# Input projections of a two-block transformer: normalisation and rotation issued between the panels, values transposed in place

## The chip, the cores and the metric

One core of a Trainium2 chip. The metric is the device time of one launch in microseconds, the median of several runs.

## What is computed

Two blocks over 256 latent tokens of width 2048. The first block has two layers; each projects the latent tokens and 256 context tokens together, and its attention has two groups of eight heads, one with grouped keys (GQA) and one with latent vectors (MLA). The second block has a gated recurrence, a causal attention and a layer of retrieved experts, and isn't touched here. The part of the reference that matters:

```python
p = h @ w_in                       # (512 tokens, 2048) @ (2048, 4672)
q, k, v, g_gqa, cq, ckv, kr, g_mla = jnp.split(p, offsets, axis=-1)
q = rms_norm(q.reshape(B, S, 8, 128), q_gain)      # per head
k = rms_norm(k.reshape(B, S, 2, 128), k_gain)
v = v.reshape(B, S, 2, 128)
qm = rms_norm(cq, cq_gain) @ w_uq                   # over 512 channels
kvm = rms_norm(ckv, ckv_gain) @ w_ukv
# latent tokens alone: q, k, the rope part of qm, and kr
q, k, kr = apply_rope(q, ...), apply_rope(k, ...), apply_rope(kr, ...)
def rms_norm(x, g):  return x * rsqrt(mean(x * x) + 1e-6) * g
def apply_rope(x):   return concat([x1 * cos - x2 * sin, x2 * cos + x1 * sin])
```

The gates `g_gqa` and `g_mla` go through silu and are multiplied into the heads' outputs.

## The kernel before

Everything is kept transposed: channels on the 128 partitions, tokens along the row. Layer 0 works on all 512 tokens. Layer 1 needs queries and gates of the latent tokens alone, so its panels of `q`, `cq` and `g` are 256 tokens wide and those of `k`, `v`, `kr` and `ckv` 512.

**A panel** is 128 output channels of a projection: 16 weight tiles of 128x128 fp32, 1 MB. To keep fp32 accuracy in the fast fp32r form, weights and inputs are split into a high and a low part, and each tile is three matmuls (`w_hi` by `h_hi`, `w_hi` by `h_lo`, `w_lo` by `h_hi`), 48 for a panel. Two halves of a panel are converted one by one: ACT rounds half m into `w_hi` (`act_half`, L1270), VectorE subtracts to get `w_lo` (`dve_half`, L1276). There are four half buffers, so half m waits until TensorE is done with half m - 4. The panels themselves lie in a ring of two slots (`SLOTS`): SyncE starts the load of the next one when the second half of the slot's holder has been subtracted.

**The order** on ACT and VectorE is set by `paced`: before it turns to output number s it converts all halves up to 2s + 4, that is the first half of panel s + 2. Then `taken` does what belongs to output s: the eviction from PSUM once TensorE is done with the panel (VectorE if it is 512 wide from token 0, ACT if not), and on VectorE some chunks of modulation. A chunk (`ada_chunk`, L1689) is a product with 2048-wide rows of another 1 MB weight, loaded by GpSimd's queue into two buffers; it takes two passes for the first 64 chunks and one for the others. `spread` says how many chunks go behind which panel.

**The input projections** of a layer are one `gemm` stage of 37 panels: 0 to 7 are q, 8 and 9 k, 10 and 11 v, 12 kr, 13 to 16 cq, 17 to 20 ckv, 21 to 36 the gates. ACT evicts a gate with Silu into one of three buffers in `sq` and stores it in DRAM at once (L1318, L1320); the stage ends when all stores have landed. Behind the last panel TensorE transposes v (L994) into a buffer that lies over the projections' input, which isn't needed any more.

**The normalisation** is a stage of its own (`norm`), begun when the three engines are done with the projections. For each of 12 groups (8 q, 2 k, cq with four tiles, ckv with four) ACT squares each tile (L1344), TensorE sums over partitions with a matmul by ones (L1026), ACT takes Ln and Exp for the reciprocal root (L1353, L1354), and VectorE scales each tile (L1797). For each of 11 groups (q, k, kr) TensorE swaps the halves of a head by a matmul (L1136), and VectorE rotates (L1763 to L1766), two groups behind the scaling. Then the attention stage begins; its first matmuls are L1154.

## Time and profile before

| what | value |
|---|---|
| median of 3 runs | 3468.65 us (3468.17 to 3477.98) |
| profiled execution | 3465.94 us, span 3464.3 us |
| busy TensorE, VectorE, ACT, GpSimd | 87%, 72%, 33%, 18% of the span |
| chain that ended last, by engine | TensorE 54%, VectorE 17%, DMA 10%, weight loads 7%, issue 6% |
| largest lines of that chain | L1008 22% (and its weight loads 7%), L955 16% |

The shares are those of the whole execution, in which the touched stages are a part. So the rows below are taken from the stretches that the change touches: the input projections of layer 0 (124 to 529 us) and of layer 1 (1052 to 1330 us) and the stage behind each. In a timeline row the first number is the start, the second the duration; a note in square brackets is the idle time before it and who ended it. In a row of the windows stand the stretch, its length, the busy us (and instructions) of TensorE, its weight loads, VectorE, ACT and GpSimd, the granted clock, the DMA share and GB/s. A row of the chain has start and duration. TensorE's rows overlap, so the step between two starts is what counts there.

### The profile page before, as it was taken

How to read it: one execution, taken by the hardware profiler on the slowest of the kernel's cores; microseconds unless marked ns; L12 is line 12 of the kernel's file. 1: busy time of each engine (PE TensorE's matmuls, PEld its weight loads, DVE VectorE, ACT ScalarE, POOL GpSimd, SP SyncE). 2: the span in 40 equal slices, each digit the busy share in tenths (PEclk: the TensorE clock that was granted, in tenths of full speed). 3: DMA queues.
4: the chain of work that ended last, by engine and by line, in shares of the span. 5: the costliest groups of instructions: out<-in, count | busy, mean ns of one | idle time of the engine just before them, and what ended most of it. 6: DMA issues, size and time to landing. Idle time of an engine off the chain costs nothing.

```text
span 3464.3 us, 39039 instructions
## 1 busy us (share of the span) xinstructions
PE 2997.7 (87%) x14684; PEld 2299.3 (66%) x14684; DVE 2501.2 (72%) x3434; ACT 1155.4 (33%) x1751; POOL 610.3 (18%) x692
## 2 busy tenths in 40 slices
PE   5899997999989997999799998799999997454555
PEld 1588884546768885659699898788888886121222
DVE  7898975555767765547664545489898997789887
ACT  1311225323233234233553635344444443111101
POOL 1000000000000000000000000122222223777773
PEclk9999999999999999999899999999999999777777
DMA  9566661343766784437444353499999999899996
GB/s 405 203 246 244 261 261 42 117 187 125 288 231 231 297 310 158 158 117 278 179 159 152 128 200 139 154 417 415 402 418 403 418 395 391 331 410 402 409 410 279
DMA packets 149477, 932.67 MB, mean 269 GB/s; under 512 B 21552, under 2 KB 30000, under 8 KB 40880
## 3 DMA queue, kind: packets, MB, share of 16 engines
q0 software_dynamic: 77568, 520.24, 38.2%
q1 hardware_dynamic: 57616, 384.82, 28.1%
q10 hardware_dynamic: 14112, 25.17, 1.9%
q8 instruction: 117, 1.92, 0.2%
q14 instruction: 64, 0.52, 0.0%
HBM read 900.79 MB, written 29.36 MB: 269 GB/s over the span
## 4 chain that ended last, share of the span: by engine, by line
PE 54%; DVE 17%; DMA 10%; PEld 7%; issue 6%; POOL 3%; ACT 3%; DVEq 0%; ACTq 0%; SPq 0%; PEldq 0%; POOLq 0%
PE psum L1008 22%; PE psum L955 16%; PEld psum L1008 7%; PE psum L1015 5%; DVE psum L2106 4%; DMA memr<-in_panels_dram 4%; PE psum L1154 3%; DVE w_lo L1276 3%; DMA memh<-dots,memr 2%; PE psum L1171 2%; DVE junk L1689 2%; POOL memh L846 1%; POOL memr L858 1%; DMA memh<-in_panels_dram 1%; PE psum L1162 1%
## 5 line engine op out<-in xcount | busy, mean ns | idle before, releaser
L1276 DVE TENSOR_TENSOR w_lo<-memr,w_hi 128x1024 fp32r<-128x1024 f32 x614 | 736.8, 1221 | 387.2 <-ACT w_hi L1270 386.4
L1270 ACT ACTIVATE w_hi<-memr 128x1024 fp32r<-128x1024 f32 x614 | 640.9, 1056 | 936.5 <-DMA memr<-in_panels_dram 321.7
L1008 PE MATMUL psum<-h_hi,w_hi 128*128 128x512 f32 (+1 forms) x1664 | 591.1, 355 | 42.7 <-DVE w_lo L1276 27.9
L1008 PE MATMUL psum<-h_lo,w_hi 128*128 128x512 f32 (+1 forms) x1664 | 578.1, 347 | 0.0
L1008 PE MATMUL psum<-h_hi,w_lo 128*128 128x512 f32 (+1 forms) x1664 | 577.9, 347 | 0.0
L1689 DVE CUSTOM_DVE_ANT_0 junk<-memr 128x2048 bf16<-128x2048 f32 x224 | 512.2, 2287 | 76.4 <-DMA memr<-in_ada_dram 55.7
L1193 PE MATMUL psum<-memr,memh 128*128 128x512 f32 x480 | 254.2, 693 | 257.0 <-ACT memh L1627 204.4
L955 PE MATMUL psum<-w_hi,l_hi 128*128 128x512 f32 x1024 | 399.7, 390 | 14.6 <-DVE w_lo L1276 14.0
L955 PE MATMUL psum<-w_hi,l_lo 128*128 128x512 f32 x1024 | 398.9, 390 | 0.0
L955 PE MATMUL psum<-w_lo,l_hi 128*128 128x512 f32 x1024 | 398.9, 390 | 0.0
L1008 PEld LDWEIGHTS psum<-h_hi,w_hi 128*128 128x128 f32 x1664 | 320.0, 192 | 93.5 <-issue 33.0
L1193 PEld LDWEIGHTS psum<-memr,memh 128*128 128x128 f32 x480 | 105.0, 224 | 405.8 <-issue 208.9
L1008 PEld LDWEIGHTS psum<-h_lo,w_hi 128*128 128x128 f32 x1664 | 320.8, 193 | 40.5 <-issue 3.1
L1008 PEld LDWEIGHTS psum<-h_hi,w_lo 128*128 128x128 f32 x1664 | 320.7, 193 | 37.8
L827 POOL DMA_DIRECT2D memr<-in_ada_dram x160 | 84.5, 528 | 1463.3 <-DVE mod L1692 1453.6
L2106 DVE SCALAR_TENSOR_TENSOR psum<-memr,memh,psum 128x2048 f32<-128x2048 f32 x130 | 306.1, 2355 | 9.6
L1008 PE MATMUL psum<-l_hi,w_hi 128*128 128x256 f32 x912 | 266.1, 292 | 20.0 <-DVE l_lo L1778 15.2
L1008 PE MATMUL psum<-l_lo,w_hi 128*128 128x256 f32 x912 | 260.4, 286 | 0.0
L1008 PE MATMUL psum<-l_hi,w_lo 128*128 128x256 f32 x912 | 260.4, 286 | 0.0
L955 PEld LDWEIGHTS psum<-w_hi,l_hi 128*128 128x128 f32 x1024 | 192.6, 188 | 56.3 <-DVE w_lo L1276 15.8
L837 POOL DMA_INDIRECT memr<-in_peer_u_dram,memr x64 | 75.9, 1186 | 863.2 <-issue 611.5
L955 PEld LDWEIGHTS psum<-w_hi,l_lo 128*128 128x128 f32 x1024 | 192.7, 188 | 39.9
(243 smaller groups left out, 4326.3 us busy)
## 6 DMA issues: line engine op xcount, KB each, us to landing
memr<-in_panels_dram SPq DMA_DIRECT2D x323, 1024.0 KB, 7.5
memr<-in_ada_dram POOLq DMA_DIRECT2D x168, 1024.0 KB, 6.0
memh<-in_panels_dram SPq DMA_DIRECT2D x16, 1024.0 KB, 23.3
dots<-sq ACTq DMA_DIRECT2D x64, 256.0 KB, 9.9
memh<-in_ada_dram POOLq DMA_DIRECT2D x8, 1024.0 KB, 16.0
memr<-in_xin_dram SPq DMA_DIRECT2D x1, 4096.0 KB, 41.6
gstore<-sq ACTq DMA_DIRECT2D x16, 256.0 KB, 3.0
memh<-gstore SPq DMA_DIRECT2D x2, 2048.0 KB, 7.3
```

The costliest lines, as they stand in the source:

```text
L827: pool.dma_start(adar[:, s_, :], ada[i * 2 + s_]).then_inc(ada_in[s_], 16)
L837: pool.indirect_dma_start(out=early_rows[:, r % EARLY_SLOTS, :], out_offset=None, in_=(peer_u if j < TOPK else peer_v)[:, :], in_offset=ba ...
L955: ins = pe.matmul(bank(2 * (group % 2) + t), x_[:, kc, t * P:t * P + P], u_[:, c, :], start=kc == 0 and j == 0, stop=kc == DC - 1 and j == 2)
L1008: ins = pe.matmul(bank(o["bank"])[:, 0:o["w"]], w_[:, c, :], x_[:, kc, :], start=kc == 0 and j == 0, stop=kc == DC - 1 and j == 2)
L1015: ins = pe.matmul(bank(o["bank"])[:, a:b], lt, rh, start=j == 0, stop=j == len(pairs) - 1)
L1154: ins = pe.matmul(b[:, 0:nk], lt, rh, start=j == 0, stop=j == len(u["s"]) - 1)
L1171: ins = pe.matmul(bank(O_BANK + u["hn"] % 2)[:, u["col"]:u["col"] + P], u["v"][c], probT[:, u["n"] % 2, c * P:c * P + P], start=c == 0, st ...
L1193: ins = pe.matmul(bank(b), diags[:, q % DIAGS, :], row_views[r % NSLOT][:, 512 * b:512 * b + 512], start=first and i == 0, stop=(EARLY + m ...
L1270: act.activation(w_hi[:, m % HALVES, :, :], slot[:, 8 * i:8 * i + 8, :], ACT.Copy).then_inc(hi_ready, 1)
L1276: dve.tensor_tensor(w_lo[:, m % HALVES, :, :], raw_panel(o["g"])[0][:, 8 * i:8 * i + 8, :], w_hi[:, m % HALVES, :, :].bitcast(F32), ALU.su ...
L1689: chain(dve.tensor_tensor_reduce(junk[:, :], w, cact[:, v_, :], 1.0, 0.0, ALU.mult, ALU.add, mod[:, a, m:m + 1]))
L2106: dve.scalar_tensor_tensor(sums_dve, row, by, sums_dve, ALU.mult, ALU.add).then_inc(row_added, 1)
```

## The change

The stage of normalisation behind the input projections is taken out, and its work is issued inside the projections, by steps (the panel's number in the stage). For a tile made in panel i: ACT squares in step i + 1, TensorE sums in step i + 2 (behind panel i + 2), ACT takes the root in step i + 3, VectorE scales in step i + 4, TensorE swaps in step i + 5 and VectorE rotates in step i + 6. The swaps follow each other one step apart, and each waits for the rotation before it. With cq and ckv the last of the four tiles counts: roots in steps 19 and 23. The root now lies in PSUM (bank 5 or 7), the sums in bank 4, the swapped half in bank 6, where it is multiplied by the sine in place.

Buffers 0 and 1 of `sq` now hold squares during the projections, so all gates go through buffer 2. The two transposes of v follow kr's panel as outputs 13 and 14 of the stage and write v over the place it comes from. Modulation chunks: in layer 0's projections 48 instead of 50, with weight 1.0 for panels 0 to 16 and 1.4 for 17 to 34, and 32 instead of 30 in its output projection. Layer 1's spread is unchanged, but kr's chunks now come behind the second transpose. ACT preloads the table set of Ln and Exp at the end of the stage.

```diff
-        spread(DC, 50, [1] * 35 + [0] * 2)
+        spread(DC, 48, [1.0] * 17 + [1.4] * 18 + [0] * 2)
-        spread(DC + 44, 30, [1] * 14 + [0] * 2)
+        spread(DC + 44, 32, [1] * 14 + [0] * 2)
...
+                        for n in range(totals["gate"], totals["gate"] + (2 if "dense" in o else 1)):
+                            gate_slot.append(n % 3 if "dense" in o else 2)
+                            gate_use.append(gate_slot[:-1].count(gate_slot[-1]))
...
+        def inside(st, groups, panels_of):
+            st["inside"] = groups
+            for step, o in enumerate(o for o in st["outs"] if "x" in o):
+                o["step"] = step
+            by_step = [o for o in st["outs"] if "x" in o]
+            swap_at = 0
+            for gr, made in zip(groups, panels_of):
+                gr.update(sq0=totals["sq"], ms=totals["ms"], sw=totals["swap"], made=[by_step[i] for i in made])
+                ready_at = made[-1]
+                if gr.get("stat", True):
+                    gr["square_at"] = [i + 1 for i in made]
+                    gr["sum_at"] = [i + 2 for i in made]
+                    gr["root_at"] = made[-1] + 3
+                    gr["scale_at"] = ready_at = made[-1] + 4
+                    totals["sq"] += len(gr["x"])
+                    totals["ms"] += 1
+                if "rope" in gr:
+                    gr["swap_at"] = swap_at = max(ready_at, swap_at) + 1
+                    gr["rope_at"] = swap_at + 1
+                    totals["swap"] += 1
...
-            v = region(HL, 4, 2, P)
+            v = region(AR + 5120, 2, 4, P)
...
+                turns = [dict(turn=[vT[:, b, P * t:P * t + P] for t in range(4)], after=[outs[-2], outs[-1]],
+                              eng="VA"[b], dst=v[:, b, :, :], view="p (t d) -> p t d", act=ACT.Copy)
+                         for b in range(2)] if kind == "kr" else []
+                return [o] + turns
...
-            norm(groups)
+            inside(st, groups, [range(i, i + 1) for i in range(10)] + [range(12, 13), range(13, 17), range(17, 21)])
...
+        SUM_BANK, SWAP_BANK = 4, 6
+        def root_of(gr):
+            return bank(5 + 2 * (gr["ms"] % 2))[:, 0:gr["x"][0].shape[-1]]
...
+        def pe_inside(pe, st, step):
+            for gr in st["inside"]:
+                for j, at in enumerate(gr.get("sum_at", ())):
+                    if at != step:
+                        continue
+                    n, w = gr["sq0"] + j, gr["x"][j].shape[-1]
+                    if j == 0 and gr["ms"]:
+                        pe.wait_ge(rinv_ready, gr["ms"])
+                    pe.wait_ge(sq_ready, n + 1)
+                    pe.matmul(bank(SUM_BANK)[:, 0:w], ones[:, :], sq[:, n % 2, 0:w], start=j == 0,
+                              stop=j == len(gr["x"]) - 1).then_inc(sq_used, 1)
+                if gr.get("swap_at") == step:
+                    if gr["sw"]:
+                        pe.wait_ge(roped, gr["sw"])
+                    if gr.get("stat", True):
+                        pe.wait_ge(normed, gr["ms"] + 1)
+                    else:
+                        pe.wait_ge(evac[gr["made"][0]["eng"]], gr["made"][0]["ev"] + 1)
+                    pe.matmul(bank(SWAP_BANK)[:, 0:S], con("swap2" if gr["pair"] else "swap", P), gr["rope"],
+                              start=True, stop=True).then_inc(swapped, 1)
...
+        def act_inside(act, st, step, chain):
+            for gr in st["inside"]:
+                for j, at in enumerate(gr.get("square_at", ())):
+                    if at != step:
+                        continue
+                    n, x = gr["sq0"] + j, gr["x"][j]
+                    act.wait_ge(evac[gr["made"][j]["eng"]], gr["made"][j]["ev"] + 1)
+                    if n >= 2:
+                        act.wait_ge(sq_used, n - 1)
+                    act.activation(sq[:, n % 2, 0:x.shape[-1]], x, ACT.Square).then_inc(sq_ready, 1)
+                if gr.get("root_at") == step:
+                    act.wait_ge(sq_used, gr["sq0"] + len(gr["x"]))
+                    if gr["ms"] >= 2:
+                        act.wait_ge(normed, gr["ms"] - 1)
+                    r = root_of(gr)
+                    chain(act.activation(r, bank(SUM_BANK)[:, 0:r.shape[-1]], ACT.Ln, bias=eps_t[:, :], scale=1.0 / gr["w"]))
+                    act.activation(r, r, ACT.Exp, scale=-0.5).then_inc(rinv_ready, 1)
...
-                if "gate" in o and o["gate"] >= 3:
-                    act.wait_ge(g_out[o["gate"] % 3], 16 * (o["gate"] // 3))
+                if "gate" in o and gate_use[o["gate"]]:
+                    act.wait_ge(g_out[gate_slot[o["gate"]]], 16 * gate_use[o["gate"]])
...
+            if "inside" in st:
+                act.preload_act_table_set("natural_log_exp_and_others")
...
+        def dve_inside(dve, st, step, chain):
+            for gr in st["inside"]:
+                if gr.get("scale_at") == step:
+                    dve.wait_ge(rinv_ready, gr["ms"] + 1)
+                    for x, gain in zip(gr["x"], gr["gain"]):
+                        ins = dve.scalar_tensor_tensor(x, x, col(*gain), root_of(gr), ALU.mult, ALU.mult)
+                    ins.then_inc(normed, 1)
+                if gr.get("rope_at") == step:
+                    x, t = gr["rope"], bank(SWAP_BANK)[:, 0:S]
+                    cos, sin = ("cos2", "sin2") if gr["pair"] else ("cos", "sin")
+                    dve.wait_ge(swapped, gr["sw"] + 1)
+                    dve.tensor_tensor(t, t, con(sin, S), ALU.mult)
+                    chain(dve.tensor_tensor(x, x, con(cos, S), ALU.mult))
+                    dve.tensor_tensor(x, x, t, ALU.add).then_inc(roped, 1)
```

## Rows read from the trace of the kernel before

**Rows 1.** Windows of the projections and the stage behind them, layers 0 and 1
```profile
124.00:529.00 405.00, 404.80 (x1780) 334.80 (x1781) 340.13 (x365) 98.14 (x115) 26.39 (x50) 1.00 0.61 230
529.00:574.00 45.00, 27.37 (x65) 11.04 (x62) 25.82 (x52) 27.18 (x45) 0.00 (x0) 0.90 0.14 53
1052.00:1330.00 278.00, 263.30 (x1729) 242.31 (x1730) 191.41 (x207) 81.15 (x98) 22.16 (x42) 0.98 0.78 297
1330.00:1371.00 41.00, 23.06 (x68) 12.84 (x66) 22.20 (x51) 21.12 (x45) 0.00 (x0) 0.87 0.23 90
```

**Rows 2.** Waits of TensorE in layer 1's projections: us, times, longest
```profile
PE psum L1008 <- DVE w_lo L1276: 16.4, 20, 3.7
```

**Rows 3.** Timeline about layer 0's normalisation stage, TensorE and ACT
```profile
528.63 1.03 PE L994 MATMUL psum<-consts,memr 128*128 128x128 f32 x8
...
531.70 1.28 ACT L1368 ACT_TABLE_LOAD   x1 [1.21 <-DMA gstore<-sq]
...
574.03 3.75 PE L1154 MATMUL psum<-memr 128*128 128x256 f32 x6 [7.45 <-DVEq L2163]
```

**Rows 4.** Timeline and chain of waits about layer 1's normalisation stage
```profile
1329.97 1.03 PE L994 MATMUL psum<-consts,memr 128*128 128x128 f32 x8
1330.64 4.43 DMA gstore<-sq
...
1371.61 5.46 PE L1154 MATMUL psum<-memr 128*128 128x512 f32 x6 [6.10 <-DVEq L2163]
```

**Rows 5.** Timeline of TensorE, sums inside the output projections of both layers
```profile
983.10 1.02 PE L918 MATMUL psum<-sq,ones 128*128 128x512 f32 x2
...
994.88 1.02 PE L918 MATMUL psum<-sq,ones 128*128 128x512 f32 x2
...
1575.43 0.59 PE L918 MATMUL psum<-sq,ones 128*128 128x256 f32 x2
...
1581.61 0.59 PE L918 MATMUL psum<-sq,ones 128*128 128x256 f32 x2
```

**Rows 6.** Chain of waits: 35 panels of layer 0, one of 256 columns
```profile
147.99 380.82 PE psum L1008 x1680
...
1814.53 5.75 PE psum L1008 x48
```

**Rows 7.** Chain of waits in layer 1's gate panels
```profile
1237.17 9.30 DMA memr<-in_panels_dram
...
1252.43 8.23 DMA memr<-in_panels_dram
1260.69 1.07 ACT w_hi L1270
1261.78 1.23 DVE w_lo L1276
1263.01 2.20 DVE junk L1689
1265.46 1.14 DVE w_lo L1276
```

**Rows 8.** Timeline of the work in layer 0's normalisation stage
```profile
541.21 0.42 DVE L1763 TENSOR_TENSOR memr<-memr,consts 128x256 f32<-128x256 f32 x1
...
542.46 0.75 DVE L1797 SCALAR_TENSOR_TENSOR memr<-memr,cols 128x512 f32<-128x512 f32 x1
```

**Rows 9.** Timeline of TensorE and ACT in layer 1's projections
```profile
1079.13 1.06 ACT L1270 ACTIVATE w_hi<-memr 128x1024 fp32r<-128x1024 f32 x1 [6.52 <-DMA memr<-in_panels_dram]
...
1094.10 0.40 PE L1008 MATMUL psum<-h_hi,w_hi 128*128 128x512 f32 x1
...
1099.42 1.06 ACT L1270 ACTIVATE w_hi<-memr 128x1024 fp32r<-128x1024 f32 x1 [8.66 <-DMA memr<-in_panels_dram]
...
1161.06 0.38 PE L1008 MATMUL psum<-h_hi,w_hi 128*128 128x256 f32 x1 [3.74 <-DVE w_lo L1276]
```

**Rows 10.** Line L1320, the stores of layer 1's gates
```profile
DMA to landing us min/median/max: 1.7/5.4/7.7
```

More of the change, by code:

```diff
@@ L307, in gemm @@
                         o["gate"] = totals["gate"]
[L308 removed]
+                        for n in range(totals["gate"], totals["gate"] + (2 if "dense" in o else 1)):
+                            gate_slot.append(n % 3 if "dense" in o else 2)
+                            gate_use.append(gate_slot[:-1].count(gate_slot[-1]))
+                        totals["gate"] = len(gate_slot)
                     o.update(g=g, n=totals["out"], bank=totals["out"] % 4, ev=totals[o["eng"]],
@@ L710, in _ @@
                     n_gates = sum("gate" in o for s_ in stages[:st["k"]] for o in s_.get("outs", ()))
-                    for i in range(3):
-                        sp.wait_ge(g_out[i], 16 * ((n_gates + 2 - i) // 3))
+                    for i in sorted(set(gate_slot[:n_gates])):
+                        sp.wait_ge(g_out[i], 16 * gate_slot[:n_gates].count(i))
                     sp.dma_start(st["x"], gstore.rearrange("p (c t) -> p c t", c=DC)[:, c0:c1, :]).then_inc(g_in, 16)
@@ L929, in pe_gemm @@
                 pe_output(pe, o, st["norm"]["groups"][0]["xl"] if p_ == 0 and "norm" in st else None)
+                if "step" in o:
+                    pe_inside(pe, st, o["step"])
                 if "sums" in st and p_ >= 2:
@@ L1129, in stats @@
                     pe_stats(pe, gr)
-            def swap(gr):
-                if gr["sw"] >= 2:
-                    pe.wait_ge(roped, gr["sw"] - 1)
-                if gr.get("stat", True):
-                    pe.wait_ge(normed, gr["ms"] + 1)
-                pe.matmul(bank(6 + gr["sw"] % 2)[:, 0:S], con("swap2" if gr["pair"] else "swap", P), gr["rope"],
-                          start=True, stop=True).then_inc(swapped, 1)
-            for i in range(len(gs) + 2):
-                if i < len(gs) and gs[i].get("stat", True):
-                    stats(gs[i])
-                if i >= 2 and "rope" in gs[i - 2]:
-                    swap(gs[i - 2])
+            for gr in gs:
+                stats(gr)
         def pe_attend(pe, st):
@@ L1284, in taken @@
                 p_ = o["n"] - st["outs"][0]["n"]
+                if "step" in o:
+                    act_inside(act, st, o["step"], chain)
                 if p_ < len(st.get("split", ())):
@@ L1300, in taken @@
                         n = o["gate"] + t
-                        if n >= 3:
-                            act.wait_ge(g_out[n % 3], 16 * (n // 3))
-                        ins = act.activation(gate_st[:, n % 3, :], bank(2 * (o["dense"] // 4 % 2) + t), ACT.Copy)
+                        if gate_use[n]:
+                            act.wait_ge(g_out[gate_slot[n]], 16 * gate_use[n])
+                        ins = act.activation(gate_st[:, gate_slot[n], :], bank(2 * (o["dense"] // 4 % 2) + t), ACT.Copy)
                     ins.then_inc(evac["A"], 1)
@@ L1316, in taken @@
                 if "store" in o:
-                    dst = gate_st[:, o["gate"] % 3, a0:a1]
+                    dst = gate_st[:, gate_slot[o["gate"]], a0:a1]
                     act.activation(dst, src, o["act"]).then_inc(evac["A"], 1)
                     act.wait_ge(evac["A"], o["ev"] + 1)
-                    act.dma_start(o["store"], dst).then_inc(g_out[o["gate"] % 3], 16)
+                    act.dma_start(o["store"], dst).then_inc(g_out[gate_slot[o["gate"]]], 16)
                     return
@@ L1335, in act_gemm @@
             if n_gates:
-                for i in range(3):
-                    act.wait_ge(g_out[i], 16 * ((n_gates + 2 - i) // 3))
+                for i in sorted(set(gate_slot[:n_gates])):
+                    act.wait_ge(g_out[i], 16 * gate_slot[:n_gates].count(i))
         def act_squares(act, gr):
@@ L1368, in act_norm @@
             act.preload_act_table_set("natural_log_exp_and_others")
-            gs = [gr for gr in st["groups"] if gr.get("stat", True)]
+            gs = st["groups"]
             def squares(gr):
@@ L1719, in taken @@
             def taken(o):
+                if "step" in o:
+                    dve_inside(dve, st, o["step"], chain)
                 if o["eng"] == "V":
@@ L1811, in scale @@
                     ins.then_inc(normed, 1)
-            for i in range(len(gs) + 2):
-                if i < len(gs) and gs[i].get("stat", True):
-                    scale(gs[i])
-                if i >= 2 and "rope" in gs[i - 2]:
-                    if gs[i - 2].get("stat", True):
-                        dve.wait_ge(normed, gs[i - 2]["ms"] + 1)
-                    rotate(dve, gs[i - 2], chain)
+            for gr in gs:
+                scale(gr)
         def dve_attend(dve, st, chain):
```

21 lines of the change are left out of this document (7 added, 14 removed).

## The prediction

> **What bounds the kernel now.** I read the page's chain first (its shares stand in the table above): matmuls of `pe_output` (L1008) lead it, so the dense projections are bound by TensorE. Then the windows of the four stretches that the change touches: the input projections of layer 0 and 1 and the normalisation stage behind each [rows 1]. In layer 0's projections TensorE is busy in 404.8 of 405 us: nothing hidden is missing there, and whatever is added to TensorE adds to the time. In layer 1's it is busy in 263.3 of 278, and the waits name who is late: `w_lo` of VectorE, 16.4 us in 20 waits [rows 2]. In the two normalisation stages no engine is full: they are a relay of small work between ACT, TensorE and VectorE.
>
> The timeline gives their length. Layer 0: the first transpose of v (the end of the last panel) starts at 528.63, attention's first matmul at 574.03, so 45.4 us [rows 3]. Layer 1: 1329.97 to 1371.61, so 41.6 us [rows 4].
>
> **What is removed.** Without the stage, attention starts when ACT has stored the last gate. In layer 0 that store had landed at 531.70, when ACT went on to the stage's table load [rows 3]; with 0.2 us for the stage's end attention would start 3.3 us behind the last panel: 45.4 - 3.3 = 42.1 us gone. In layer 1 the store is issued at 1330.64 and takes 4.43 us [rows 4], so 5.3 us behind: 36.3 us gone. Sum 78.4 us.
>
> **What TensorE gets between the panels.** A sum of squares 512 wide inside a stream of panels can be seen in layer 0's output projection: sums at 983.10 and 994.88, a period of 11.78 us [rows 5]. A panel of 512 columns without one is 380.82 / 35 = 10.88 us [rows 6]. So 0.90 us for each. With 256 columns: period 6.18, plain panel 5.75 or 5.76 [rows 5, 6], so 0.42. A swap (256 wide, also fp32) isn't seen in a stream; I take the same 0.42, with bounds 0.3 and 0.9.
> Layer 0: 18 sums x 0.90 = 16.2; 11 swaps x 0.42 = 4.6; 8 transposes of v, which were hidden behind the last gate's store and now lie between panels, 1.0 [rows 3]. Together 21.8 us. Layer 1: 8 + 4 sums x 0.42 = 5.0; 2 + 4 sums x 0.90 = 5.4; swaps 4.6; transposes 1.0. Together 16.0 us; 1.8 of it (the sums of steps 21, 22) falls where TensorE waits anyway, so 14.2.
>
> **The new waits.** At the end of each panel `pe_inside` waits: the sum of panel s-2 for the root that ACT computes in step s, and the swap for the rotation that VectorE does in step s. Both engines do that behind the conversion of half 2s+4, which is the first half of panel s+2 and can't begin before panel s is half through. Before, TensorE could be some 1.5 panels ahead of the conversions; now it can't leave panel s before half 2s+4 is converted. Queued behind the waiting matmul is the whole next panel.
> The chain from mid-panel: round 1.07, subtract 1.14 to 1.23 [rows 7], the rotation, from 541.21 to 542.46 us three operations that overlap to 1.25 [rows 8], handovers 0.3: 3.8 to 4.3 us, and another 0.7 if the scaling comes first. In layer 0 half a panel is 5.44 us: it fits with about a microsecond over, if VectorE is free. There it does two subtractions 2.4, an eviction 0.7 (taken like the 0.75 of a scaling [rows 8]), scaling and rotation 2.0, and 1.14 modulation chunks per panel. One pass is 2.45 us from start to next start [rows 7], two passes 4.8, so 5.5: 10.6 of the 12.2 us that a panel now takes. Before it had 1.43 chunks; the lighter first weights are what makes this fit. Rounding gives panels 3, 10, 17 and 18 two chunks. Only panel 10's meets a swap: in step 11 VectorE comes to its subtractions 9.0 us into the panel and ends the rotation at 13.2, against 10.88: a stall of 2.3 us. ACT was busy in 98 of 405 us [rows 1] and gets some 2 us a panel more: not full. Bounds 0 and 8.
> The two chunks moved to layer 0's output projection (one pass each) cost 4.9 us of VectorE over 14 panels. It works there (2.4 + 1.0 + 5.5 + 0.9) of 11.78 us, so nothing; uncovered, 4.9.
> **Layer 0: -42.1 + 21.8 + 2.3 = -18.0 us.**
>
> **Layer 1** is tighter, because a query panel is 5.76 us and half of it, 2.88, is less than the 4-us chain. The panel ring has two slots, too: a load goes out when the second half of a panel is subtracted, lands in 8.23 or 9.30 us, then round 1.07, subtract 1.23, chunk 2.45, subtract 1.14 [rows 7]: 14.2 us for two panels, 15.3 at 9.30. In the query panels this ring already lags behind TensorE: panel 8 starts at 1094.10, but ACT rounds half 18 (step 7's) at 1099.42, having waited for the panel's load [rows 9]. Today that is free, since the wide panels behind let it catch up. With the new waits TensorE pays it. I moved the stretch step by step, with panel loads of 7 to 8.4 us. Step 4: half 12's load is there at 1079.13 as before [rows 9], rounded at 1080.2, square 0.4, root 0.9, so 1081.5; panel 4, two sums of 0.42 later than before, ends at 1077.7: stall 3.8. Step 6: its panel ends at 1094.4, the rotation (half 16 subtracted at 1093.9) at 1095.2: 0.8. Step 7: panel's end 1101.9; half 18's load, begun at 1091.5, lands at 1099.9, rounded, subtracted and rotated 1103.4: 1.5. So 6.1 us up to panel 8. Among the wide panels 8 to 11 the chain fits. Into step 12 VectorE comes late by panel 11's three chunks (7.4 and some 3 for their loads): 2.8. In step 13 it has two more chunks and half 30 first and rotates 10.9 us after panel 13 began, which takes 5.8: 5.1. Steps 14 and 15, alike with one chunk and none: 0.7 and 1.9. Against that the `w_lo` wait of 3.74 us in panel 14, 5.5 with what follows from it [rows 9], goes: the two transposes are outputs of their own, `paced` converts one more half ahead of the first, and the chunks hang on the second. So 6.1 + 10.5 - 5.5 = 11.1 us to panel 17. Bounds: 0 - 5.5, if loads land early, and 25, if they land at 9 us.
> In the gate panels the ring is the bound [rows 7], so each delay of VectorE or ACT shows. Step 23 gives ACT a root and two table loads (1.28 each [rows 3]), step 24 gives VectorE four scalings, 2.7. Some 1.4 us of the first is slack: I take 3.
> The gates now use one buffer of `sq` instead of three, so each waits until the one before has landed. In layer 1 a store lands in 1.7 to 7.7 us, median 5.4 [rows 10], and gates are some 6.8 us apart with 0.8 of it gone for eviction and issue. About a quarter of the stores are late, by up to 1.7: I take 1, and 1.5 more at the end, where two gates come close together. In layer 0 gates are 10.9 us apart: nothing.
> **Layer 1: -36.3 + 14.2 + 11.1 + 3 + 2.5 = -5.5 us.**
>
> On the switches between Silu and Ln the row shows 1.28 us for a load and work right behind it. The Trainium skill (ScalarE: Activation LUTs, What ACT_TABLE_LOAD costs) speaks against the change here: it gives about 2.66 us for each switch, with a drain, and its section on table sets says to batch calls by set, which the change breaks up. By that rule layer 1 would lose 2.8 us more; by the rows it loses what I took.
>
> **Clock.** In the two removed stretches the granted clock was 0.90 and 0.87 of full, against 1.00 and 0.98 in the projections before them [rows 1]. So attention now starts behind dense work at 2.4 GHz, not behind a sparse stretch partly at 1.2: 0.5 us for each layer, an estimate between 0 and 2.
>
> **Sum.** -18.0 - 5.5 - 1.0 = -24.5 us. The profiled execution took 3465.94 us (span 3464.3), 2.7 under the median of 3468.65, so 3441.4 on its scale and 3444.2 on the median's: 3444.
>
> **The rivals.**
> *A: the new waits are free, 0.2.* The ring recovers in the longer panels, and VectorE's order hides the rotations. Layer 0: -42.1 + 21.8 = -20.3. Layer 1: -36.3 + 14.2 - 5.5 + 3 = -24.6. With the clock -46, so 3423, or up to 3432 with a few stalls. For it: VectorE was busy in only 191 of 278 us of layer 1's projections [rows 1]. Against it: a half panel of 2.88 us can't hold a 4-us chain.
> *B: layer 1 gives back all of the gain, 0.17.* If loads land at 9 us all along, its stalls are 25 instead of 11 and the gate panels lose 5 more: -24 + 14 + 5 = -5, so 3464, or from 3452 on with half of it. For it: loads of 8.23 and 9.30 us in the chain [rows 7]. Against it: the added 14 us of TensorE work are themselves slack for the loads.
> *C: slower than before, 0.04.* The single gate buffer decides. If stores in layer 1 landed later than (6.8 - 0.8) = 6.0 us as a rule, each of 15 gates would pay the excess and the kernel would be tied to store, evict, store. From a landing of 7.6 us on, 1.6 x 15 = 24 eats the gain; at 8.5 it is 2.5 x 15 = 38, and 3444 + 38 = 3482. For it: a longest landing of 7.7 [rows 10]. Against it: the median is 5.4.
> *D: the change doesn't do what it says, 0.02:* a stage is still waited for. 3468.
>
> The forecast keeps 0.57. Range: 3425 (most of A) to 3459 (half of B); what is left out is the rest of both, C and D, 0.2. A difference of 0.3% (10.4 us, about what a measurement can tell) lies at 3458.2: faster 0.84, same 0.12, slower 0.04.
>
> **What would show it.** In the profile after: no L1026 or L1136 row behind the last panel of either layer; attention's first matmul 3 to 4 us behind layer 0's last panel, 5 to 7 behind layer 1's; panels with a sum 0.90 or 0.42 us longer; in layer 1 waits of the new matmuls for ACT's root and VectorE's rotation in steps 4, 6, 7 and 12 to 15, of 15 to 20 us in all, and no wait of 3.74 in panel 14; layer 0's with one such wait of 2 us near step 11. I am wrong if these waits are missing (A), or if the last gate of layer 1 ends more than 35 us later than before relative to its first panel (B, C).

## The result and the profile after

The changed kernel took 3450.37 us (median of 4 runs, 3446.20 to 3451.03) against 3470.86 (3468.17 to 3477.98): ratio 0.9934, 95% interval 0.9921 to 0.9946, so 23 us or 0.66% less; 3444 within 3425 to 3459 was forecast. The profiled execution took 3450.2 us (span 3448.5, before 3464.3).

Windows of the changed kernel: layer 0's projections and what lies between them and attention, then layer 1's from its panel 1 on (columns as in [rows 1]).
```profile
124.00:554.00 430.00, 427.71 (x1842) 346.70 (x1842) 360.82 (x411) 126.32 (x162) 25.34 (x48) 0.99 0.56 212
554.00:557.00 3.00, 0.45 (x1) 0.45 (x2) 0.00 (x0) 1.70 (x2) 0.00 (x0) 0.92 0.23 87
1036.80:1344.00 307.20, 284.66 (x1794) 257.77 (x1794) 212.53 (x258) 103.41 (x144) 22.18 (x42) 0.97 0.70 268
1344.00:1351.00 7.00, 0.32 (x2) 0.23 (x2) 0.00 (x0) 1.67 (x2) 0.00 (x0) 0.82 0.60 239
```
The stretches of 45 and 41 us of [rows 1] have shrunk to 3 and 7. In layer 0's projections TensorE is still busy in all but 2.3 us, with more instructions in a longer stretch. In layer 1's it is idle for 22.5 of 307.2 us, where it was for 14.7 of 278, and the granted clock is 0.97 where it was 0.98.

The waits of TensorE from panel 1 of layer 1 to attention name who is late (us, times, longest), to be laid beside [rows 2]:
```profile
PE psum L1058 <- DVE w_lo L1315: 13.0, 16, 3.2
PE psum L952 <- DVE memr L1837: 8.2, 6, 2.8
PE psum L1193 <- ACTq L1736: 6.7, 1, 6.7
PE psum L943 <- ACT psum L1335: 3.1, 1, 3.1
```
Two waits are new: the swap (L952) for VectorE's rotation, and a sum of squares (L943) for ACT's root. The waits for `w_lo` fell by 3.4: the one of 3.74 us in panel 14 [rows 9] isn't there.

Timeline of TensorE, starts of attention in layers 0 and 1:
```profile
556.55 3.66 PE L1193 MATMUL psum<-memr 128*128 128x256 f32 x6 [2.83 <-ACTq L1736]
...
1350.78 2.07 PE L1193 MATMUL psum<-memr 128*128 128x512 f32 x2 [6.68 <-ACTq L1736]
```
From the first projection matmul to attention layer 0 went from 449.8 us (124.2 to 574.03) to 432.1 (124.47 to 556.55): -17.7, forecast -18.0. From panel 1 to attention layer 1 went from 319.4 (1052.25 to 1371.61) to 314.0 (1036.79 to 1350.78): -5.4, forecast -5.5. Attention of layer 1 starts 20.8 us earlier. That is 2.3 less than the two gains together: the first projection matmul comes 0.3 later, and from layer 0's attention to panel 1 of layer 1 it takes 480.2 us instead of 478.2. Of these 2.0 us 1.7 lie in one place. In both kernels TensorE waits 2.02 us behind layer 0's first heads; the 10 us after it read, in the kernel before and in the changed one:
```profile
641.00:651.00 10.00, 9.95 (x23) 4.48 (x24) 1.89 (x3) 2.78 (x5) 0.00 (x0) 1.00 0.00 1
```
```profile
623.50:633.50 10.00, 10.00 (x20) 4.35 (x21) 1.89 (x3) 2.29 (x5) 0.00 (x0) 0.83 0.00 0
```
The granted clock is 1.00 in the one and 0.83 in the other, behind the same wait. Why isn't shown.

The profiled execution ends 15.8 us earlier, so 5 more us came back behind layer 1's attention, in work that is the same in both. VectorE's instructions there, laid side by side, are 21.1 us earlier at 2219 us of the kernel before, 19.4 at 2971 and 15.7 at the end: most of it goes in the last 500 us. These are two single executions; the two medians differ by 20.5, and the ratio gives 23. The cause was not traced.

The new waits are visible one by one. VectorE and then TensorE at the end of layer 1's step 12:
```profile
1145.15 2.29 DVE L1751 CUSTOM_DVE_ANT_0 junk<-memr 128x2048 bf16<-128x2048 f32 x1 [3.41 <-DMA memr<-in_ada_dram]
...
1147.62 2.35 DVE L1315 TENSOR_TENSOR w_lo<-memr,w_hi 128x1024 fp32r<-128x1024 f32 x2
1149.89 0.42 DVE L1835 TENSOR_TENSOR psum<-psum,consts 128x256 f32<-128x256 f32 x1
...
1150.67 0.42 DVE L1837 TENSOR_TENSOR memr<-memr,psum 128x256 f32<-128x256 f32 x1
```
```profile
1151.14 1.22 PE L952 MATMUL psum<-memr,consts 128*128 128x256 f32 x2 [2.83 <-DVE memr L1837]
1152.16 1.91 PE L1044 MATMUL psum<-consts,memr 128*128 128x128 f32 x8
1153.72 0.56 PE L1058 MATMUL psum<-h_hi,w_hi 128*128 128x256 f32 x1
```
Read it downwards: VectorE waits 3.41 us for a chunk's load, does the chunk of step 11, then both subtractions of step 12, and only then the rotation; TensorE stands 2.83 us before the swap. And the swap takes 1.22 us here. In layer 0, without a wait ahead of it, the same two instructions read:
```profile
282.54 0.59 PE L952 MATMUL psum<-memr,consts 128*128 128x256 f32 x2
282.97 1.04 PE L1044 MATMUL psum<-consts,memr 128*128 128x128 f32 x8
```
Behind this wait TensorE works at 1.2 GHz instead of 2.4. That price wasn't in the forecast.

### The profile page after: what moved, and what is told of

Read it like the earlier page. It is cut to its first block, busy times and chain, and to the rows that moved or that the text cites. A ratio compares the mean times of both kernels' runs of the same rounds, so it can differ in the third digit from the quotient of the medians.

```text
span 3448.5 us, 39045 instructions
## 1 busy us (share of the span) xinstructions
PE 2988.6 (87%) x14684; PEld 2303.8 (67%) x14684; DVE 2498.5 (72%) x3434; ACT 1160.9 (34%) x1757; POOL 605.8 (18%) x692
## 4 chain that ended last, share of the span: by engine, by line
PE 55%; DVE 17%; DMA 10%; PEld 7%; issue 5%; POOL 3%; ACT 2%; DVEq 0%; ACTq 0%; SPq 0%; PEldq 0%; POOLq 0%
PE psum L1058 22%; PE psum L1005 16%; PEld psum L1058 7%; PE psum L1065 6%; DVE psum L2181 4%; DMA memr<-in_panels_dram 4%; DVE w_lo L1315 4%; PE psum L1193 3%; DVE junk L1751 2%; DMA memh<-dots,memr 2%; PE psum L1210 2%; DMA memh<-in_panels_dram 1%; POOL memr L884 1%; POOL memh L872 1%; PE psum L1201 1%
## 5 line engine op out<-in xcount | busy, mean ns | idle before, releaser
L1058 PE MATMUL psum<-h_hi,w_hi 128*128 128x512 f32 (+1 forms) x1664 | 605.0, 364 | 39.5 <-DVE w_lo L1315 24.7
L1005 PE MATMUL psum<-w_hi,l_hi 128*128 128x512 f32 x1024 | 400.0, 391 | 15.3 <-DVE w_lo L1315 14.7
L2181 DVE SCALAR_TENSOR_TENSOR psum<-memr,memh,psum 128x2048 f32<-128x2048 f32 x130 | 306.1, 2355 | 10.7 <-DVE psum L2181 1.4
L1058 PE MATMUL psum<-l_hi,w_hi 128*128 128x256 f32 x912 | 266.5, 292 | 19.4 <-DVE l_lo L1858 14.7
L1005 PEld LDWEIGHTS psum<-w_lo,l_hi 128*128 128x128 f32 x1024 | 192.8, 188 | 40.2
## 6 DMA issues: line engine op xcount, KB each, us to landing
memh<-in_panels_dram SPq DMA_DIRECT2D x16, 1024.0 KB, 23.6
```

What stands on the lines that cost most here:

```text
L1005: ins = pe.matmul(bank(2 * (group % 2) + t), x_[:, kc, t * P:t * P + P], u_[:, c, :], start=kc == 0 and j == 0, stop=kc == DC - 1 and j == 2)
L1058: ins = pe.matmul(bank(o["bank"])[:, 0:o["w"]], w_[:, c, :], x_[:, kc, :], start=kc == 0 and j == 0, stop=kc == DC - 1 and j == 2)
L2181: dve.scalar_tensor_tensor(sums_dve, row, by, sums_dve, ALU.mult, ALU.add).then_inc(row_added, 1)
```

## The experiments

"Inside work" stands for all that the change inserts between the panels: squares, sums, roots, scalings, swaps and rotations. The first column of numbers is the ratio to the kernel before, on the same chip; the second is the distance of that ratio from the changed kernel's 0.9934, times 3470 us (the two 95% intervals together make it uncertain by 6 to 8 us, so a distance of less says nothing by itself); the third is when layer 1's attention starts in the profiled execution, against 1350.78. The last four runs were on a chip on which the kernel before took 3511 to 3515 us, so only ratios go across.

| run | ratio (95%) | us from the changed kernel | layer 1's attention, us |
|---|---|---|---|
| changed kernel | 0.9934 (0.9921 to 0.9946) | 0 | 1350.78 |
| inside work first, both engines | 0.9883 (0.9869 to 0.9898) | -17.7 | -14.2 |
| no inside work | 0.9782 (0.9768 to 0.9796) | -52.7 | -51.0 |
| old weights of layer 0's chunks | 0.9965 (0.9953 to 0.9977) | +10.8 | +10.2 |
| three gate buffers | 0.9928 (0.9915 to 0.9941) | -2.1 | -2.8 |
| transposes late | 0.9929 (0.9915 to 0.9942) | -1.7 | +0.2 |
| fewer chunks in layer 1 | 0.9923 (0.9909 to 0.9937) | -3.8 | +3.0 |
| gates without Silu | 0.9930 (0.9916 to 0.9944) | -1.4 | 0.0 |
| together | 0.9895 (0.9880 to 0.9910) | -13.5 | -13.6 |
| VectorE's inside work first | 0.9905 (0.9891 to 0.9919) | -10.1 | -9.8 |
| ACT's inside work first | 0.9937 (0.9924 to 0.9949) | +1.0 | -1.1 |
| thin spread | 0.9866 (0.9851 to 0.9881) | -23.6 | -17.8 |
| best | 0.9854 (0.9836 to 0.9872) | -27.8 | -25.9 |

**What the inside work costs.**
```diff
-            for gr, made in zip(groups, panels_of):
+            for gr, made in ():
```


> The squares, sums, roots, scalings, swaps and rotations of queries, keys and latent vectors are left out; nothing takes their place, so attention works on vectors that are neither normalised nor rotated. The two transposes and the gate buffer stay as they are. This measures what the inserted work and its waits cost together. Theory (my terms): layer 0 20.8 for the matmuls and 1.8 for the stall, layer 1 13.2 and 11 + 3 for waits: 50 us less than the changed kernel, 3400 us. Rival (part of the inserted work in layer 1 fills time in which TensorE would wait for the panel ring): waits for w_lo grow by 8 us or more and the time is 3408 to 3415.

3394.8 us, with normalisation and rotation left out altogether. In the trace layer 0 is 23.3 us shorter (408.8 from first matmul to attention), against 22.6 by my terms. Together with layer 1, attention there starts 51.0 us earlier; expected was 50. TensorE's waits in layer 1:
```profile
PE psum L1058 <- DVE w_lo L1315: 18.4, 18, 4.6
PE psum L1193 <- ACTq L1736: 7.1, 1, 7.1
```
Waits for `w_lo` do grow (18.4 against 13.0), as the rival had it, yet not enough to eat the gain. The longest, 4.6 us, stands in panel 14, where the kernel before has its 3.74, although the transposes of v lie ahead of it.

**The order inside a step.** The squares, roots, scalings and rotations of a step are issued ahead of the two conversions of the step.
```diff
-        def paced(st, part, taken):
+        def paced(st, part, taken, first=None):
...
             for o in st["outs"]:
+                if first is not None and "step" in o:
+                    first(o["step"])
                 while j < min(2 * split + (5 if "x" in o else 4), len(halves_)):
...
-                if "step" in o:
-                    act_inside(act, st, o["step"], chain)
```
(and the same on VectorE; `first` calls `act_inside` and `dve_inside`.)

> The order on ACT and VectorE alone is changed: in each step squares, roots, scalings and rotations come before the two half-panel conversions of the step, not behind them. Theory (the stalls of the new matmuls come from standing behind the conversion of half 2s+4): the 1.6 us wait in layer 0's step 11 goes, and of the 11.3 us of waits for the root and the rotation in layer 1's steps 4, 6 to 8 and 12 to 16 at least 8 go; 3439 to 3443 us against 3450. Rival (in layer 1 the ring of panel loads is late anyway): the same time comes back as waits for the subtracted half (w_lo), the sum of TensorE's waits in layer 1's projections stays within 3 us of what it was, 3447 to 3450. Second rival: ACT, which now first waits for the end of a panel, converts halves later, and the time grows to 3453 or more.

3432.0 us against 3469.65: 17.7 us less, more than the theory's 7 to 11. Waits of TensorE from panel 1 of layer 1 on:
```profile
PE psum L1058 <- DVE w_lo L1317: 12.0, 13, 2.3
...
PE psum L952 <- DVE memr L1837: 5.4, 3, 4.0
```
The wait for the root is gone, the waits for the rotation fell from 8.2 to 5.4, and layer 0's from 1.55 to none. That is 5.9 us in layer 1 where at least 8 were expected, as one of 4.0 us, in step 13, is new. Yet from panel 1 to panel 17 layer 1 takes 139.8 us instead of 149.8, 10.0 less for 5.9 of waits: they had cost more than their length.

Each engine's half alone:

> Of the order that gave 3432 us only VectorE's half: scalings and rotations come ahead of its two subtractions, while ACT squares and takes roots behind its conversions as in the changed kernel. Theory (the rotation behind the subtraction of half 2s+4 is the larger part of the stalls): the waits for VectorE of 8.2 us in layer 1 and 1.6 in layer 0 fall to under 3, the wait of 3.1 us for ACT's root in step 4 stays, 9 to 13 us less than the changed kernel: 3437 to 3441. Rival (the lateness sits on ACT, whose conversions VectorE waits for in either order): 5 us less at most, 3445 or more.

> The other half alone: squares and roots ahead of ACT's conversions, VectorE as in the changed kernel. Theory: the 3.1 us wait of step 4 and part of the 3.2 us wait for w_lo behind step 23's root go, the waits for the rotation stay; 3 to 6 us less: 3444 to 3447. Rival (ACT's order is the larger part): 9 us less or more, 3441 or below.

Waits in layer 1 with VectorE's inside work first, and then with ACT's:
```profile
PE psum L952 <- DVE memr L1838: 5.0, 3, 4.0
PE psum L943 <- ACT psum L1337: 3.3, 1, 3.3
```
```profile
PE psum L1058 <- DVE w_lo L1317: 12.9, 15, 3.0
PE psum L952 <- DVE memr L1838: 12.6, 6, 3.6
```
VectorE's half gives 10 of the 18 us, as expected, though its waits for the rotation fell to 5.0 and not under 3. ACT's half alone gives nothing that can be told (0.9937), where 3 to 6 us were expected and 9 by its rival: the root comes in time, but VectorE then stands behind the same subtractions, and a wait of 3.6 us for the rotation, at the end of step 6, takes the place of the 3.1 for the root. The lateness is passed on: moving ACT's work ahead gains only where VectorE's is ahead too (attention of layer 1 starts 4.4 us earlier with both than with VectorE's alone).

**The chunks ahead of a rotation in layer 0.**
```diff
-        spread(DC, 48, [1.0] * 17 + [1.4] * 18 + [0] * 2)
+        spread(DC, 50, [1] * 35 + [0] * 2)
-        spread(DC + 44, 32, [1] * 14 + [0] * 2)
+        spread(DC + 44, 30, [1] * 14 + [0] * 2)
```


> Only the spread of layer 0's modulation chunks is put back to what it was before (50 chunks evenly over 35 panels, 30 in the output projection). Panels 5, 8, 10 and 12 then have two chunks and are followed by a swap. Theory (VectorE with two chunks ends the rotation 13 us into a panel of 10.9): stalls of 1.6 to 2.3 us in steps 6, 9, 11 and 13 instead of in step 11 alone, layer 0 longer by 5 to 7 us: 3455 to 3457. Rival (a late rotation in one step is made up by slack, or the two chunks in the output projection cost as much): no difference, within 2 us of the changed kernel. Second rival (with 1.43 chunks a panel VectorE is full and its lag adds up): 10 us or more, 3460.

10.8 us slower than the changed kernel, attention of layer 0 at 567.41. Waits of TensorE in layer 0's projections:
```profile
PE psum L952 <- DVE memr L1837: 7.4, 4, 2.7
PE psum L943 <- ACT psum L1335: 2.5, 1, 2.5
```
The four waits for the rotation are where the theory put them (steps 6, 9, 11, 13: 1.6, 1.6, 1.6, 2.7). A fifth, 2.5 us for the root in step 3, nobody had forecast, and the waits' 9.9 us against 1.6 cost 10.9. So the size lies at the second rival's, its mechanism (a lag that adds up) isn't seen. The run changes the number of chunks (50 for 48) together with their weights, so it doesn't tell which of the two counts.

**The chunks ahead of a rotation in layer 1.**
```diff
-        spread(DC + 44, 32, [1] * 14 + [0] * 2)
-        spread(DC + 60, 42, [0.6] * 8 + [2] * 5 + [0.6] * 4 + [2] * 4 + [0.8] * 14 + [0] * 2)
+        spread(DC + 44, 38, [1] * 14 + [0] * 2)
+        spread(DC + 60, 36, [1, 0, 1, 1, 0, 1, 1, 0, 2, 2, 2, 1] + [0] * 4 + [1, 2, 2, 3, 2] + [1] * 14 + [0] * 2)
```


> Six modulation chunks are taken out of layer 1's input projections (panels 7 and 11 to 15: two, one, one, none, none, none there instead of more) and put into layer 0's output projection, 38 instead of 32 over 14 panels. Theory (VectorE comes late to the rotations because of the chunks ahead of them): the waits of 2.8 us in step 12 and 2.5 in step 14 go, 4 to 6 us less: 3444 to 3447, and layer 0's output projection, with 11.0 us of VectorE in 11.8, pays nothing. Rival (the stalls come from the order behind the conversion, whatever VectorE does in between; or VectorE is full in the output projection): within 2 us of the changed kernel, or slower.

Waits of TensorE in layer 0's output projection and the first pair of layer 1 (850 to 1050 us), and then of the swap in layer 1's projections:
```profile
PE psum L1058 <- DVE w_lo L1315: 9.4, 6, 2.3
```
```profile
PE psum L952 <- DVE memr L1837: 3.6, 5, 0.7
```
The time can't tell this run from the changed kernel, and layer 1's attention starts 3.0 us later. In layer 1 alone the theory holds: no wait for a rotation over 0.72 us, and from panel 1's `w_lo` wait to attention it takes 308.9 us instead of 314.0. But the place I moved the chunks to wasn't free: the changed kernel has 1.9 us of such waits between 850 and 1050, this one 9.4, and layer 1 begins 8.1 us later. My sum of 11.0 us of VectorE in 11.8 counted VectorE's work and left out its waits for the chunks' loads: from 850 to 1000 us they are 32.2 us, against 22.6 in the changed kernel.

**The transposes.** They go back behind the last panel.
```diff
-                turns = [dict(turn=[vT[:, b, P * t:P * t + P] for t in range(4)], after=[outs[-2], outs[-1]],
...
             st = gemm(g, 37, in_proj)
+            add(st, [dict(turn=[vT[:, b, P * t:P * t + P] for t in range(4)],
+                          after=[o for o in st["outs"] if o["g"] - g in (10, 11)],
```

> The two transposes of the values stand behind the last gate panel again (as before the change, but still in place); all else is the changed kernel. The prediction held that moving them ahead takes away the 3.74 us wait of layer 1's panel 14 (one more half is converted ahead, the chunks hang on the second transpose). By that theory the wait returns: 3.7 to 5.5 us more in layer 1, less the 1 us of transposes in each layer that hide behind the last store again: 3452 to 3454. Rival: the run without the inside work had a wait of 4.61 us at that place although the transposes stood ahead, so it is the waits for the rotation in steps 12 to 15 that took its place; then nothing returns, and the time is that of the changed kernel or up to 2 us less: 3448 to 3451.

The rival's case: 0.9929, and no wait for `w_lo` of 3.74 us in panel 14. The waits of layer 1:
```profile
PE psum L1059 <- DVE w_lo L1316: 13.9, 17, 3.3
PE psum L953 <- DVE memr L1838: 9.7, 6, 2.8
```
The 3.74 us aren't removed by the place of the transposes.

**The gate buffers.**
```diff
-                            gate_slot.append(n % 3 if "dense" in o else 2)
+                            gate_slot.append(n % 3 if "dense" in o else o["slot"])
...
-                    o.update(store=..., eng="A", act=ACT.Silu)
+                    o.update(store=..., eng="A", act=ACT.Silu, slot=2 if i < 3 else i % 3)
```


> The gates from the fourth on use all three buffers again (by then no squares are left), the first three the single one. Theory (the last gates of layer 1 are tied to store, eviction, store): ACT's waits for a gate's store, 12 us in 4 waits, go but for those of the first gates, attention starts 5.5 us after the end of the last panel instead of 7.5, and the waits for w_lo in the gate panels shrink by 1 to 3 us: 3 to 5 us in all, 3445 to 3447. Rival (only the last store counts, and it lands no earlier): within 1 us of the changed kernel.

The end of the chain of waits before layer 1's attention in the changed kernel (start, duration):
```profile
1329.31 7.07 DMA gstore<-sq
...
1336.82 4.88 DMA gstore<-sq
...
1342.13 6.42 DMA gstore<-sq
...
1348.99 1.70 DMA gstore<-sq
```
Store, eviction, store, four times. With three buffers ACT waits for TensorE there, not for a store:
```profile
1343.28 0.38 ACT L1378 ACTIVATE sq<-psum 128x256 f32<-128x256 f32 x1 [6.08 <-PE psum L1058]
```
Attention starts 2.8 us earlier in the trace. The ratio (2.1 us less, give or take 6) can't tell that from nothing; the place and the mechanism are shown, the size is just below the theory's 3 to 5.

**The table loads.**
```diff
-                    o.update(store=..., eng="A", act=ACT.Silu)
+                    o.update(store=..., eng="A", act=ACT.Copy)
```


> The gates are stored without Silu (Copy in its place), so ACT never leaves the table set of Ln and Exp in the projections; attention then multiplies by the raw projection. This takes the three table loads of step 23 in each layer and those at the first gate and at the end away: 5 of 1.28 us for each layer. Theory (ACT is late at step 23 and TensorE waits 3.2 us for the half that it converts next): that wait shrinks to under 1 us, 2 to 4 us less, all of it in layer 1: 3446 to 3448. Rival (a slower ring alone makes that wait): within 1 us. By the Trainium skill (ScalarE: Activation LUTs, What ACT_TABLE_LOAD costs), at 2.66 us a switch, it would be 4 to 6 us.

ACT about layer 1's step 23, changed kernel:
```profile
1256.98 1.28 ACT L1334 ACT_TABLE_LOAD   x1
1258.28 0.66 ACT L1334 ACTIVATE psum<-psum,eps_t 128x512 f32<-128x512 f32 x1
1258.96 1.28 ACT L1335 ACT_TABLE_LOAD   x1
1260.25 0.58 ACT L1335 ACTIVATE psum<-psum 128x512 f32<-128x512 f32 x1
1260.85 1.28 ACT L1378 ACT_TABLE_LOAD   x1
...
1262.99 1.06 ACT L1309 ACTIVATE w_hi<-memr 128x1024 fp32r<-128x1024 f32 x1 [0.46 <-ACT sq L1378]
1264.52 1.06 ACT L1309 ACTIVATE w_hi<-memr 128x1024 fp32r<-128x1024 f32 x1 [0.48 <-DMA memr<-in_panels_dram]
```
and without Silu:
```profile
1258.95 1.06 ACT L1309 ACTIVATE w_hi<-memr 128x1024 fp32r<-128x1024 f32 x1 [0.46 <-ACT sq L1378]
1264.19 1.06 ACT L1309 ACTIVATE w_hi<-memr 128x1024 fp32r<-128x1024 f32 x1 [4.17 <-DMA memr<-in_panels_dram]
```
Three loads, not two: one also between Ln and Exp. Without them ACT converts a half 4.0 us earlier, and then waits 4.17 us for the next panel's load, which lands at the same time. TensorE's wait of 3.21 us falls to 1.57, and one of 3.04 appears half a dozen microseconds later. Attention starts at 1350.74 against 1350.78. The rival is right: the panel loads alone set this stretch.

**Parts together, and the best version.** First the order on both engines, three gate buffers, the six chunks moved as above, and the table set loaded by hand ahead of the root:

> The inside work ahead of the conversions on ACT and VectorE, three buffers for the gates from the fourth on, the six chunks moved from layer 1 to layer 0's output projection, and the table set of Ln and Exp loaded by hand ahead of the root of step 23 (one load less there). With the order alone the time was 3432. Theory (the parts add up): 3 us for the gates, 3 to 4 for the one wait of 3.97 us for a rotation that was left in layer 1, 0 to 1 for the table: 3424 to 3427. Rival (the ring of panel loads is now the bound of layer 1 and takes each gain back): 3430 or more. Floor: 3394.8 without the inside work, plus 20.8 and 15.0 of TensorE for it, is 3431, less what fills waits for the ring.

0.9895, no better than the order alone (0.9883, intervals overlap), so 6 to 9 us above the theory's: from panel 1's `w_lo` wait to attention layer 1 takes 293.6 us instead of 302.6, but the output projection has 10.0 us of `w_lo` waits, and that wait stands 9.7 us later. So the chunks had to go elsewhere:
```diff
-        spread(DC, 48, [1.0] * 17 + [1.4] * 18 + [0] * 2)
-        spread(DC + 44, 32, [1] * 14 + [0] * 2)
+        spread(DC, 50, [1.0] * 17 + [1.6] * 18 + [0] * 2)
+        spread(DC + 44, 34, [1] * 14 + [0] * 2)
+        spread(DC + 60, 38, [1, 0, 1, 1, 0, 1, 1, 1, 2, 2, 2, 2, 0, 0, 1, 0, 1, 2, 2, 3, 1] + [1] * 14 + [0] * 2)
```


> The order of 3432 us on both engines and three buffers for the gates; of layer 1's 42 modulation chunks only four are moved (none in panels 12, 13 and 15), two of them into layer 0's gate panels (50 chunks there) and two into its output projection (34 over 14 panels). Six more in the output projection had brought 9.4 us of waits for w_lo there and delayed layer 1 by 8 to 10 us. Theory (those waits begin only where the output projection gets more than about 2.4 chunks a panel): no such waits here, the 3.97 us wait of layer 1 gone, 3424 to 3428. Rival (any chunk more delays the panel loads of the output projection): 3430 to 3434.

0.9866 is 3424 us on the scale of 3470, as the theory had it. Between 850 and 1050 us the `w_lo` waits are 2.2 us: 34 chunks fit in the output projection, 38 don't. Layer 0's gate panels pay instead:
```profile
PE psum L1058 <- DVE w_lo L1317: 5.5, 4, 4.0
```
Last, 48 chunks there as in the changed kernel, 34, and 40 in layer 1:

> The order of the 3432-us kernel on both engines, three buffers for the gates, layer 0's input projections again with 48 chunks as in the changed kernel, 34 in its output projection and 40 in layer 1's (none in panels 12, 13 and 15). The run before had 50 chunks in layer 0's input projections, which cost 5.5 us of waits for w_lo in its gate panels and 9 us over the panels in all. Theory: that goes and layer 1 keeps its gain, attention of layer 1 starts near 1325 us, and the ratio to the kernel before falls from 0.9866 to between 0.983 and 0.985, which is 3411 to 3418 us on the scale of 3470. Rival (the two chunks put back into layer 1, in steps 4 and 20, bring waits there): 0.986 to 0.988.

0.9854, just outside the 0.983 to 0.985 expected, with attention of layer 1 at 1324.93 as forecast. The ratios of this run and the last can't be told apart; attention starts 8.1 us earlier. Its waits from panel 1 of layer 1 on:
```profile
PE psum L1058 <- DVE w_lo L1317: 12.6, 13, 2.3
...
PE psum L952 <- DVE memr L1837: 0.6, 1, 0.6
```
This version beats the kernel before by 1.46% (interval 1.28 to 1.64), twice what the change gave.

It also prices the waits. Both kernels have the same inserted matmuls in steps 1 to 16 of layer 1. The changed kernel takes 149.8 us for them (panel 1 at 1036.79, panel 17 at 1186.58), this one 132.0 (1033.22 to 1165.20): 17.8 us for 10.7 us of waits. The rest is TensorE's own time for the same work: it is busy for 138.6 us in the one and 131.4 in the other. Windows of steps 12 and 13, changed kernel from the end of the 2.83-us wait, then the best version:
```profile
1151.10:1162.30 11.20, 10.44 (x59) 9.94 (x60) 10.49 (x15) 2.64 (x4) 1.05 (x2) 0.72 0.68 273
```
```profile
1127.60:1140.10 12.50, 12.50 (x59) 10.23 (x58) 9.54 (x13) 4.18 (x5) 1.06 (x2) 1.00 0.45 182
1140.10:1152.40 12.30, 12.30 (x103) 12.22 (x102) 8.96 (x13) 4.66 (x8) 0.00 (x0) 1.00 0.59 230
```
Steps 12 and 13 take 25.5 us in the one (1136.83 to 1162.35) and 18.7 in the other (1127.59 to 1146.24). The waits are 2.83 and 0.72, so 3.3 us more are the clock: granted 0.72 over the 11 us behind the wait, against 1.00.

That is not the price of every wait. In the run with the transposes late the swap of step 12 also waits 2.82 us, and it takes 0.70 us, with a granted clock of 0.85 over the next 11 us; in layer 0 with the old weights a wait of 2.70 us is followed by 1.00. What decides it isn't shown.

## Why the prediction was right

The time, the split between the layers and the mechanism came out. Inside layer 1 several terms were wrong and cancelled, so it is luck that its sum holds to 0.1 us.

- **What is removed** (42.1 and 36.3): attention starts 3.0 us behind the last panel of layer 0 (542.68 + 10.88 to 556.55), forecast 3.3, and 6.8 behind that of layer 1 (its last matmul starts at 1343.8 and is done by 1344.0), forecast 5.3 + 1.5. Right.
- **What TensorE gets**: panels with a sum take 11.78 and 6.18 us, with a swap too 12.22, so 0.90, 0.42 and 0.44. The swap was taken by analogy, and held. Without inside work layer 0 is 23.3 us shorter, against 20.8 + 1.8.
- **Layer 0's stall**: in step 11, as forecast, and the only one; 1.55 us of wait and 1.8 of time, against 2.3. That the new spread carries this is shown by the old one: 10.8 us more.
- **Layer 1's stalls up to panel 17.** Forecast 16.6 us of new waits, less 5.5 for the wait in panel 14. Measured from the start of panel 1 to that of panel 17: 125.4 us before (1052.25 to 1177.63), 149.8 after, so +24.4. Of TensorE's forecast 14.2 us, 11.6 lie there (ten sums of 0.42, two of 0.90, eleven swaps, the transposes), so 11.6 + 11.1 = 22.7 was forecast, and the net stall is 12.8 instead of 11.1. Inside it the terms moved. Steps 4, 6 and 7: 3.06, 0.72, 0.72 where I had 3.8, 0.8, 1.5. Step 12: 2.83 for 2.8. Step 13: 0.72 for 5.1, the term that failed. VectorE ended that rotation 8.2 us behind the start of panel 13, not 10.9, and the panel, at the lower clock, took 7.6, not 5.8. Steps 14 and 15: 2.48 and 0.72 for 0.7 and 1.9. The waits add up to 11.3, not 16.6, and those that went are 4.2, not 5.5. What the forecast lacked is the clock behind the waits: TensorE is busy for 138.6 us there and was for 121.2, 17.4 more for 11.6 us of inserted work, so 5.8 us (7 against the best version, above). Two errors of opposite sign.
- **The wait of panel 14** did go, but my reason ("`paced` converts one more half ahead, and the chunks hang on the second transpose") fell. Without inside work it is back, 4.6 us, with the transposes ahead; with the transposes late it doesn't return. It goes when TensorE is held up elsewhere in steps 12 to 15, or, in the best version, when one chunk lies in panels 12 to 15 instead of four. That the ring then catches up is my reading of the two; no run shows the ring alone.
- **Gate panels and buffer** (3 + 1 + 1.5): from panel 17 to attention 164.2 us against 194.0 before, so -29.8; my terms give -36.3 + 2.6 + 5.5 = -28.2. The panels themselves take 157.4 us against 152.3, so 5.0 more, where 2.6 + 3 + 1 = 6.6 was forecast. The six sums there are 4.4 by themselves, with the 1.8 that I took as hidden, and the `w_lo` waits are 11.1 us, 10.6 before; how the 5.0 divides isn't shown. The root's table loads were taken as the reason for part of the 3 us, and cost nothing: without Silu attention starts at the same time. By the rule of the Trainium skill (ScalarE: Activation LUTs, What ACT_TABLE_LOAD costs) each switch should have cost about 2.66 us. The trace shows 1.28 us each with work right behind, and no time at all in this place.
- **Clock** (-1): attention's first 8 us are granted 0.79 instead of 0.73 in layer 0, and 0.73 instead of 0.67 in layer 1, so it doesn't start at full clock either way; in layer 0 its first 67 us are 0.1 us shorter, not 0.5. The gain I booked was smaller than two losses that I hadn't: those 5.8 us, and the 1.7 us behind layer 0's first heads.
- **The rivals.** A (the waits are free) is refuted by 10 to 18 us that the order alone gives back. B (layer 1 gives all back) didn't happen: the net stall up to panel 17 is 12.8 us, not 25, and the gate panels lost nothing to speak of. C's mechanism, store, eviction, store, is there at the very end of layer 1 and costs 2.8 us, not 15 gates' worth. D (a stage is still waited for) is out: of 45 and 41 us, 3 and 7 are left.

## What to carry to other kernels

When small dependent work is woven into a stream of big matmuls, try it ahead of the bulk conversions in each engine's queue, on every engine of the relay at once: here one half alone gave 10 of 18 us and the other nothing. A wait of a busy TensorE can cost more than its length, so look at the granted clock behind it. Before moving filler work to an engine that looks free on average, count the loads that it brings and what they make wait: here six chunks more in the output projection brought 7.5 us of waits for `w_lo`.

## What the hardware showed unexpectedly

- A wait of TensorE of 2.83 us between dense panels was followed by work at 1.2 GHz: the swap took 1.22 us instead of 0.59, eight transposes 1.91 instead of 1.04, and the granted clock over the next 11 us was 0.72. In layer 1's steps 1 to 16 waits of 10.7 us cost 17.8. Waits of 2.82 and 2.70 us in other runs were followed by 0.85 and 1.00.
- Behind one and the same wait of 2.02 us, the next 10 us were granted 1.00 in the kernel before and in the run with the transposes late, and 0.83 in all others: 1.7 us.
- ACT loaded a table between Ln and Exp of one root when it came from Silu (1.28 us each, three loads in step 23).
- The kernel before took 3470 us on one chip and 3511 to 3515 on another; layer 1's attention starts at 1349.72 us there with ACT's work first, and at 1350.78 here in the changed kernel, so the difference arises in the later stages. Only ratios were compared across them.
